# Own transfer for the first scale vector, down weights in two transfers per expert, and activations grouped by half and kind

## What is computed

```python
u = rms_norm(h, norm1_g); proj = u @ w_in                 # w_in: 1024 x 4608
y_conv = conformer_conv(proj[..., :1024], ...)
y_attn = moba_attention(q, k, v, q_norm_g, k_norm_g) @ w_attn_out
g = sigmoid(proj[..., c4:] + b_gates)
h = h + (g[..., :D] * y_conv + g[..., D:] * y_attn) @ w_out
u2 = rms_norm(h, norm2_g); top_v, top_i = top_k(u2 @ w_router + b_router, 4)
# for each expert e and the tokens routed to it:
    t = u2[tok] @ w_ug[e] + b_ug[e]                       # 1024 -> 2048
    a = minimum(t[:, :1024], 7); lin = clip(t[:, 1024:], -7, 7)
    act = a * sigmoid(1.702 * a) * (lin + 1)
    h[tok] += gate * (act @ w_down[e] + b_down[e])        # 1024 -> 1024
```

## Time and profile before

| | us |
|---|---|
| median of three runs | 1130.43 |
| lowest and highest | 1129.95, 1130.46 |
| the profiled execution's own time | 1127.98 |
| its span | 1126.2 |
| PE busy | 967.3 |
| DVE busy | 393.8 |
| ACT busy | 309.8 |

### The profile page before, as it was taken

How to read it: one execution, slowest core, us unless ns; L and a number is a source line. 1 busy time by engine, 2 the same in 40 slices (tenths; PEclk the granted TensorE clock), 3 DMA queues, 4 the chain that set the end, 5 groups by cost and what they waited for, 6 DMA issues and landing times.

```text
span 1126.2 us, 19760 instructions
## 1 busy us (share of the span) xinstructions
PE 967.3 (86%) x7261; PEld 445.8 (40%) x7262; DVE 393.8 (35%) x1014; ACT 309.8 (28%) x534; POOL 5.3 (0%) x27
## 2 busy tenths in 40 slices
PE   6999899998666769899996799998996976998667
PEld 5998689632211213233331233332332321332112
DVE  4699966432111112223232133322322321232111
ACT  4565573222111111212221122221221211222111
POOL 1000000000000000000000000000000000000000
PEclk8999999999888898999998899998999998999887
DMA  7473259999999999999999999999999999999996
GB/s 270 169 290 122 103 182 402 387 414 425 425 427 426 427 428 426 427 425 426 427 427 425 428 425 426 425 428 425 426 425 427 427 426 427 426 427 429 425 427 250
DMA packets 50918, 432.97 MB, mean 384 GB/s; under 512 B 4845, under 2 KB 5265, under 8 KB 18128
## 3 DMA queue, kind: packets, MB, share of 16 engines
q1 hardware_dynamic: 50424, 432.50, 92.3%
q10 hardware_dynamic: 472, 0.16, 0.1%
HBM read 431.59 MB, written 1.05 MB: 384 GB/s over the span
## 4 chain that ended last, share of the span: by engine, by line
PE 48%; DMA 24%; SPq 20%; DVE 4%; issue 2%; ACT 1%; DVEq 0%; ACTq 0%
PE bank L1312 16%; SPq L404 12%; DMA up_odd<-in_w_up_gate 10%; DMA up_even<-in_w_up_gate 10%; PE bank L1043 9%; PE bank L1346 8%; SPq L410 6%; PE bank L1234 5%; DMA down_even<-in_w_down 3%; PE bank L1303 3%; PE bank L1281 2%; DVE up_odd L723 2%; PE bank L1073 1%; PE bank L1332 1%; DVE w_lo L698 1%
## 5 line engine op out<-in xcount | busy, mean ns | idle before, releaser
L1312 PE MATMUL bank<-up_even,reg_r 128*32 128x512 f32 x1472 | 189.9, 661 | 68.2 <-DMA up_even<-in_w_up_gate 68.2
L1312 PE MATMUL bank<-up_odd,reg_r 128*32 128x512 f32 x1408 | 179.4, 654 | 66.1 <-DMA up_odd<-in_w_up_gate 66.1
L998 DVE TENSOR_TENSOR ys<-reg_m,ys 64x512 fp32r<-64x512 f32 x90 | 61.7, 685 | 236.6 <-ACT ys L650 236.0
L1312 PEld LDWEIGHTS bank<-up_even,reg_r 128*32 128x32 f32 x1472 | 47.0, 115 | 203.6 <-DMA up_even<-in_w_up_gate 103.9
L1312 PEld LDWEIGHTS bank<-up_odd,reg_r 128*32 128x32 f32 x1408 | 44.9, 115 | 194.0 <-DMA up_odd<-in_w_up_gate 99.1
L638 ACT ACTIVATE reg_m<-reg_m 128x256 f32<-128x256 f32 x45 | 18.9, 420 | 370.4 <-DVE reg_m L979 370.4
L1234 PE MATMUL bank<-reg_h,reg_r 128*32 128x256 f32 x736 | 93.2, 636 | 0.7 <-DVE reg_r L869 0.7
L979 DVE TENSOR_SCALAR reg_m<-bank 128x256 f32<-128x256 f32 x45 | 19.1, 425 | 211.7 <-PE bank L1312 211.7
L646 ACT ACTIVATE reg_m<-bank,gslot 128x512 f32<-128x512 f32 x45 | 30.9, 688 | 195.5 <-PE bank L1346 195.5
L1346 PE MATMUL bank<-down_even,reg_r 128*32 128x512 f32 x736 | 84.4, 596 | 0.4
L1346 PE MATMUL bank<-down_odd,reg_r 128*32 128x512 f32 x704 | 80.7, 596 | 0.5 <-DMA down_odd<-in_w_down 0.5
(11 more groups left out here) (252 smaller groups left out, 1188.1 us busy)
## 6 DMA issues: line engine op xcount, KB each, us to landing
up_even<-in_w_up_gate SPq DMA_DIRECT2D x64, 2048.0 KB, 35.8
up_odd<-in_w_up_gate SPq DMA_DIRECT2D x64, 2048.0 KB, 38.5
down_even<-in_w_down SPq DMA_DIRECT2D x64, 1024.0 KB, 36.5
down_odd<-in_w_down SPq DMA_DIRECT2D x64, 1024.0 KB, 36.5
down_even<-in_w_in SPq DMA_DIRECT2D x6, 2048.0 KB, 8.4
down_odd<-in_w_in SPq DMA_DIRECT2D x2, 2048.0 KB, 8.7
down_odd<-in_w_in SPq DMA_DIRECT2D x4, 512.0 KB, 8.5
down_odd<-in_w_attn_out SPq DMA_DIRECT2D x1, 2048.0 KB, 8.0
```

The source lines that it names most:

```text
L998: ins = nc.vector.tensor_tensor(ys[64:P, half, :], YR[r, :], ys[0:64, half, :].bitcast(F32), ALU.subtract)
L1312: ins = mm(UP[q * SLOTS:(q + 1) * SLOTS, :], XT[:, k % 2, k // 2 * SLOTS:(k // 2 + 1) * SLOTS], up_columns(a, k, q), start=False, stop=(k ...
```

## The change

It has five parts.

1. norm1_g goes straight into a tile of its own, g1c, 8 values per partition, by the first transfer of ACT's queue, with its own semaphore. The tile par keeps the other eight transfers; four of them are issued behind the pieces of group 0, and PE's transposes and DVE's copies of them move behind group 0's first half.
2. Feature 8p + k lies at partition p, position k: w_in is loaded so (eight neighbouring rows per partition), and x is transposed with a stride of 8.
3. Only the first 256 columns of group 0 stay plain fp32. The other 256 are split into high and low parts and use the three products.
4. Four neighbouring rows of the down weights lie on one partition. In the loop they come as two transfers of 2 MB, 16 KB per partition; for the first two experts still as four of 1 MB.
5. In UP, partitions 0 to 63 hold the first 1024 columns (two groups of 512) and partitions 64 to 127 the linear half. The elementwise steps run over 64 partitions by 512, the sigmoid's result goes to UP in PSUM, and PE transposes four blocks of which half the columns are used.

The diff, without unchanged lines and without the renumbered columns of par:

```diff
@@ -50,6 +50,8 @@
+DOWNS = 2
+DOWNK = KD // DOWNS
@@ -147,9 +149,10 @@
-        ACT_A, ACT_B, ACT_C = [REG_M[:, 256 * i:256 * i + 256] for i in range(3)]
+        ACT_AC = REG_M[:, 0:512]
+        ACT_A, ACT_C = ACT_AC[0:64, :], ACT_AC[64:P, :]
-        actT = REG_R[:, 896:1152].rearrange("p (j s) -> p j s", j=2)
+        actT = REG_R[:, 896:1152].rearrange("p (r s) -> p r s", r=4)
@@ -203,17 +207,18 @@
...
+        ACT_B = UP[0:64, :]
         def up_columns(a, k, q):
-            return up[a][:, k, :].rearrange("p (g f) -> p g f", g=2)[:, :, 256 * q:256 * q + 256]
+            return up[a][:, k, 512 * q:512 * q + 512]
@@ -265,7 +270,7 @@
-        win = w_in.rearrange("(k p) n -> p k n", p=P)
+        win = w_in.rearrange("(p k) n -> p k n", k=KD)
@@ -330,18 +335,12 @@
-            sp.dma_start(dwr, conv_dw).then_inc(par_in, 16)
-            sp.dma_start(rows[8:24, :], b_gates.rearrange("(r c) -> r c", c=P)).then_inc(par_in, 16)
-            for r, src in ((36, q_norm_g), (37, k_norm_g)):
-                sp.dma_start(rows[r:r + 1, :].rearrange("r (h d) -> r h d", h=2),
-                             src.rearrange("(r h d) -> r h d", r=1, h=1).to_broadcast([1, 2, HD])).then_inc(par_in, 16)
-            def down_part(a, c):
-                return (DOWN_EVEN, DOWN_ODD)[a][:, 2 * D * c:2 * D * c + 2 * D]
+            def down_part(a, c, n):
+                return (DOWN_EVEN, DOWN_ODD)[a][:, n * c:n * c + n]
@@ -349,8 +348,9 @@
             def load_down(a, c, e):
-                sp.dma_start(down_part(a, c), w_down[e, 2 * c * P:(2 * c + 2) * P, :].rearrange("(p r) n -> p (r n)", r=2)
-                             ).then_inc(down_in[a][c], 16)
+                h, r = c // 2, c % 2 * 2 * D
+                sp.dma_start(down_part(a, c, 2 * D), w_down[e, DOWNK * h * P:DOWNK * (h + 1) * P, :].rearrange("(p r) n -> p (r n)", r=DOWNK)[:, r:r + 2 * D]
+                             ).then_inc(down_in[a][h], 16)
@@ -358,13 +358,17 @@
+                    sp.dma_start(dwr, conv_dw).then_inc(par_in, 16)
+                    sp.dma_start(rows[0:16, :], b_gates.rearrange("(r c) -> r c", c=P)).then_inc(par_in, 16)
+                    for r, src in ((28, q_norm_g), (29, k_norm_g)):
+                        sp.dma_start(rows[r:r + 1, :].rearrange("r (h d) -> r h d", h=2),
+                                     src.rearrange("(r h d) -> r h d", r=1, h=1).to_broadcast([1, 2, HD])).then_inc(par_in, 16)
                     for q in range(4):
-                        sp.dma_start(bup[q * E:(q + 1) * E, :].rearrange("e (g f) -> e g f", g=2),
-                                     b_up_gate.rearrange("e (g h f) -> e g h f", g=2, h=4)[:, :, q, :]).then_inc(bup_in, 16)
+                        sp.dma_start(bup[q * E:(q + 1) * E, :], b_up_gate[:, 512 * q:512 * q + 512]).then_inc(bup_in, 16)
@@ -405,9 +409,9 @@
             def fetch_down(a, e, items):
-                for c in range(4):
+                for c in range(DOWNS):
-                    sp.dma_start(down_part(a, c), w_down[bass.ds(e, 1), 2 * c * P:(2 * c + 2) * P, :].rearrange("e (p r) n -> p (e r n)", r=2)
+                    sp.dma_start(down_part(a, c, DOWNK * D), w_down[bass.ds(e, 1), DOWNK * c * P:DOWNK * (c + 1) * P, :].rearrange("e (p r) n -> p (e r n)", r=DOWNK)
@@ -476,7 +480,8 @@
-            for r, src, n in ((0, norm1_g, 8), (24, conv_dw_b, 4), (28, conv_ln_g, 4), (32, conv_ln_b, 4)):
+            act.dma_start(g1c[:], norm1_g.rearrange("(p k) -> p k", k=KD)).then_inc(g1_in, 16)
+            for r, src, n in ((16, conv_dw_b, 4), (20, conv_ln_g, 4), (24, conv_ln_b, 4)):
@@ -495,9 +500,14 @@
             def weights_high(i, b):
-                arrived(act, i)
+                if i == 0:
+                    for c in range(4):
+                        act.wait_ge(g0_in[c], 16)
+                else:
+                    arrived(act, i)
+            weights_high(0, 1)
@@ -638,10 +648,10 @@
-                nc.scalar.activation(actT, ACT_T[:, 0:2 * P].rearrange("p (j s) -> p j s", j=2),
+                nc.scalar.activation(actT, ACT_T[:].rearrange("p (r s) -> p r s", r=4)[:, :, 0:2 * SLOTS],
-                act.wait_ge(down_done[3], n + 1)
+                act.wait_ge(down_done[DOWNS - 1], n + 1)
@@ -671,13 +681,9 @@
-            dve.wait_ge(par_full, 1)
-            nc.vector.tensor_copy(par[:], PAR_BANK[:, 0:38]).then_inc(par_ready, 1)
-            nc.vector.tensor_copy(dwT[:], PAR_BANK[:, 64:64 + KC * TAPS].rearrange("p (c w) -> p c w", c=KC)).then_inc(par_ready, 1)
-            dve.wait_ge(par_ready, 2)
+            dve.wait_ge(g1_in, 16)
@@ -694,13 +700,19 @@
-                dve.wait_ge(w_hi_ready, 2 * (i - 1) + b + 1)
+                dve.wait_ge(w_hi_ready, 2 * i + b)
-            for i in (1, 2):
-                for b in range(2):
-                    weights_low(i, b)
+            weights_low(0, 1)
+            for b in range(2):
+                weights_low(1, b)
+            dve.wait_ge(par_full, 1)
+            nc.vector.tensor_copy(par[:], PAR_BANK[:, 0:30]).then_inc(par_ready, 1)
+            nc.vector.tensor_copy(dwT[:], PAR_BANK[:, 64:64 + KC * TAPS].rearrange("p (c w) -> p c w", c=KC)).then_inc(par_ready, 1)
+            for b in range(2):
+                weights_low(2, b)
+            dve.wait_ge(par_ready, 2)
@@ -976,8 +988,8 @@
-                nc.vector.tensor_scalar(ACT_A, UP[:, 0:256], LIMIT, None, ALU.min).then_inc(clip_ready, 1)
-                nc.vector.tensor_scalar(ACT_C, UP[:, 256:512], LIMIT, -LIMIT, ALU.min, ALU.max).then_inc(lin_ready, 1)
+                nc.vector.tensor_scalar(ACT_A, UP[0:64, :], LIMIT, None, ALU.min).then_inc(clip_ready, 1)
+                nc.vector.tensor_scalar(ACT_C, UP[64:P, :], LIMIT, -LIMIT, ALU.min, ALU.max).then_inc(lin_ready, 1)
@@ -1022,14 +1034,9 @@
-                        ins = nc.tensor.transpose(bank[(U_XT + b) % 4][:, c:c + P], hx[:, m, k * P:(k + 1) * P], ident[:])
+                        ins = nc.tensor.transpose(bank[(U_XT + b) % 4][:, c:c + P], features(m)[:, k, :], ident[:])
-            pe.wait_ge(par_in, 16 * 9)
-            nc.tensor.transpose(PAR_BANK[:, 0:38], rows, ident[0:38, 0:38])
-            for c in range(KC):
-                ins = nc.tensor.transpose(PAR_BANK[:, 64 + c * TAPS:64 + (c + 1) * TAPS], dwr[:, c * P:(c + 1) * P], ident[0:TAPS, 0:TAPS])
-            ins.then_inc(par_full, 1)
@@ -1061,19 +1068,22 @@
-            for b in range(2):
-                u = U_G + b
-                claim(u)
-                for c in range(2):
-                    ch = 2 * b + c
-                    for k in range(KD):
-                        if ch == 0 and k % 2 == 0:
-                            freed(pe, U_XT + k // 2)
-                            pe.wait_ge(g0_in[k // 2], 16)
-                        ins = mm(bank[u % 4][:, c * T:(c + 1) * T], stream[0][1][:, k, ch * P:(ch + 1) * P], uT[:, k, :],
-                                 start=(k == 0), stop=(k == KD - 1))
-                ins.then_inc(bank_full[u % 4], 1)
+            claim(U_G)
+            for c in range(2):
+                for k in range(KD):
+                    if c == 0 and k % 2 == 0:
+                        freed(pe, U_XT + k // 2)
+                        pe.wait_ge(g0_in[k // 2], 16)
+                    ins = mm(bank[U_G % 4][:, c * T:(c + 1) * T], stream[0][1][:, k, c * P:(c + 1) * P], uT[:, k, :],
+                             start=(k == 0), stop=(k == KD - 1))
+            ins.then_inc(bank_full[U_G % 4], 1)
+            pe.wait_ge(par_in, 16 * 8)
+            nc.tensor.transpose(PAR_BANK[:, 0:30], rows, ident[0:30, 0:30])
+            for c in range(KC):
+                ins = nc.tensor.transpose(PAR_BANK[:, 64 + c * TAPS:64 + (c + 1) * TAPS], dwr[:, c * P:(c + 1) * P], ident[0:TAPS, 0:TAPS])
+            ins.then_inc(par_full, 1)
+            channel_group_bank(0, 1)
@@ -1328,8 +1338,8 @@
-                for j in range(2):
-                    ins = nc.tensor.transpose(ACT_T[:, j * P:(j + 1) * P], ACT_A.rearrange("p (f j) -> p j f", j=2)[:, j, :], ident[:])
+                for r in range(4):
+                    ins = nc.tensor.transpose(ACT_T[:, r * P:(r + 1) * P], ACT_AC.rearrange("p (f r) -> p r f", r=4)[:, r, :], ident[:])
@@ -1338,13 +1348,14 @@
-                for c in range(4):
-                    pe.wait_ge(down_in[a][c], 16 * pair + 16)
-                    for j in range(2):
+                for c in range(DOWNS):
+                    pe.wait_ge(down_in[a][c], 16 * pair + 32)
+                    for r in range(DOWNK):
                         for half in range(2):
-                            row = (2 * half + j) * SLOTS
-                            ins = mm(YB[row:row + SLOTS, :], actT[:, j, c * SLOTS:(c + 1) * SLOTS],
-                                     down[a][:, 2 * c + j, half * 512:(half + 1) * 512], start=(c == 0), stop=(c == 3), skip_group_check=True)
+                            row = (2 * half + r % 2) * SLOTS
```

(3 more changed lines are left out.)

19 lines of the change are left out of this document (10 added, 9 removed).

## The result

The changed kernel takes 1118.89 us, the median of four runs (1118.4 to 1119.93), against 1130.19 for the kernel before, four runs beside it (1129.8 to 1130.46): ratio 0.9908, 95% interval 0.9889 to 0.9927, so 8.3 to 12.5 us less. The forecast was 1121.7 with a range from 1118.8 to 1127.0; the time lies inside it, 0.1 us from its lower edge. The profiled execution took 1118.4, span 1116.7, which is 9.6 us under the profiled execution before (1127.98), where the sum said 8.7. A later comparison with more runs gave less: 1119.72 (six runs, 1116.93 to 1123.11) against 1127.53 (eleven runs, 1125.71 to 1133.89), ratio 0.9919 [0.9891, 0.9947]. The ratios rest on all the executions and need not be the quotients of the medians: here the medians differ by 7.8 us, the ratio says 9.1 (6.0 to 12.3).

What follows compares the result with a forecast made beforehand. It took a front bound by the chain of engines, then some 900 us bound by expert-weight delivery. Terms -4.8 - 4.2 + 0.3 = -8.7 gave 1119.3 profiled, 1121.7 against the median of 1130.43; range 1118.8 to 1127.0.

Steps and rivals of the forecast that it cites:

- the sum: Whole kernel: -4.8 for the front, -4.2 for the weight stream, +0.3 for the last tile, together -8.7 us.
- The opening: Front of the kernel: group 1 starts at 25.0 instead of 29.8 us, gaining 4.8 us, bounds 2.7 to 5.2.
- The rival that w_in's new order makes it land later: Front: w_in's new row order lands later; with the low-clock case 2.1 to 2.5 us lost, 1124, together 13%.
- The clock question: Group 0's plain half: if PE's clock stays low until 18.0 us, the front gains 2.7 us, not 4.8.
- the removed wait: Opening: PE no longer waits for the last parameter vector; scale copy at about 8.7 us, 4.15 us earlier.
- the half in three products: Second half of group 0: 48 fp32r matmuls take 5.8 us in place of 7.0.
- The stream: Down weights in the expert loop: 16 KB runs save 0.13 to 0.15 us per expert, 30 experts, 4.2 us.
- The upper bound of 6.3: Down weights: 126 MB at 419 against 428 GB/s from the DMA windows, 300 less 294 us.
- The estimate of 1.7 us: Down weights: about 3 overhead cycles per packet, 3 in 256 beats against 3 in 512, 0.6% of down time.
- The tile: Expert loop: DVE chain 1.04 us longer but covered; four transposes add 0.2 to 0.34 us per tile, hidden by the queue.
- Near 724: End of the multi-tile experts' run: 4.1 us of queued work, 1.7 remaining after the change, so nothing is lost.
- The end: Last tile: the added transposes stand open once, costing 0.3 us.

Runs made afterwards that it cites:

- wait_par: Changed kernel with parameter transfers, transposes and copies ahead of group 0 again, norm1_g keeping its own transfer; 1121.26 us, ratio 0.9945 to the kernel before.
- after_again: The changed kernel run once more without edit beside the kernel before; 1119.72 us, ratio 0.9919.
- runs8: Changed kernel with its 2 MB down transfers cut into two of 1 MB with 8 KB runs; 1123.16 us, ratio 0.9954 to the kernel before.
- big8: Kernel before plus parts 1 to 3, down weights in two 2 MB transfers per expert with 8 KB runs; 1124.51 us, ratio 0.9972.
- tile_1: Changed kernel with one unused 512-column fp32 multiply more per tile, 0.86 us; 1123.22 us, ratio 0.9958 to the kernel before.
- front_only: Kernel before plus parts 1 to 3 alone, down rows and column groups as before; 1122.65 us, ratio 0.9959.
- up2: Changed kernel with the loop's up weights in two 4 MB transfers of 32 KB runs, not four of 2 MB; 1120.09 us, ratio 0.9934 to the kernel before.
- g0_plain: Changed kernel with part 3 undone, all of group 0 as plain fp32 multiplies; 1119.85 us, ratio 0.9931 to the kernel before.

## Why the prediction was right

**The opening** went as worked out. Scale copy 8.92 (said 8.7), u_lo done at 17.06 (16.7), w_lo at 19.26 (19.1), second half of group 0 from 19.36 to 25.1 (19.2 to 25.0), group 1 at 25.0 (25.0). Two readings in it were too short and did no harm. PE's first multiply came 0.75 later than said (10.36, not 9.6): it follows the start of the scalings by 0.98, as it did before (13.31 to 14.29 in the earlier trace rows), and 0.45 had been allowed; the 1.44 us of waiting for w_lo took this up. And 0.8 was put for two matmuls whose row says 1.22; the copy came only 0.2 late, as they could start at 7.75. The last piece of group 0 landed at 12.27 (13.1 said). In four of the ten traces PE waited 0.4 to 1.2 us for such a piece, always ahead of the wait for w_lo, so it stayed hidden. The rival that w_in's new order makes it land later falls: group 1 landed at 20.82 where it had 20.70 before, and in eight of the ten traces at 20.9 or earlier.

The clock question came out on the good side by luck: the prediction put all 16 multiplies at the upper pace, though before the first 3.7 us had the lower, and gave no reason for it. The 16 multiplies took 7.14 (as t = 0.44 said) or ran at that pace with a wait in between in nine of the ten traces, and 9.97 in wait_par. Of the prices of the parts, that of the removed wait is read from the traces, 2.5 to 3.9 us at the first up multiply; that of the half in three products is not told apart from nothing. And the 4.8 is rather low than high: nine of the ten traces reach the first up multiply 4.4 us or more earlier than the kernel before, and after_again 4.0; the median of the ten is 5.4.

**What was not foreseen** is 0.5 us at the end of the routing: the lead was still 4.8 us at 213 and 5.3 at the first up multiply. Before, PE's granted clock was 0.66 from 215 to 220; after, it was 1.00 in that stretch. Nothing of the change acts there, and other traces scatter by more.

**The stream**: 4.2 said, 4.65 measured in landings (30 x 0.155), and confirmed by runs8 and big8 as a price of the run. The term was undersized by a tenth since PE's starts gave 9.93 and 9.80 and the landings give 9.94 and 9.79. The upper bound of 6.3 from the windows' 419 and 428 GB/s was not reached; a window of 8 us counts packets by their starts and is a rougher measure than the landings. The estimate of 1.7 us that the prediction worked out from the Trainium skill (DMA: Bandwidth & Descriptors, section Why small descriptors are slow) is too small here by more than half; the traces have 10 to 12.5 ns per run.

**The tile**: four transposes take 0.25 us more (1101.29 to 1101.88, 0.59 against 0.34 in the earlier trace rows), between the 0.2 and 0.34 said, and the longer chain on DVE stayed covered: in the tile at 626 us the last product ended at 629.1, PE's gather at 629.9. Tiles now follow at 15.85 us, 15.60 before. Near 724 2.7 us of work were left, 1.7 said. The error was to the safe side, in part because the tiles grew by 0.25 and not by 0.34. That it did not matter is luck in part as well: the margin rests on PE's clock behind the last landing, which in tile_1 took 2.0 us of such a margin by itself.

**The end**: +0.3 said, +0.49 in the trace. The transposes are 0.25 of it. The rest is PE's pace in the last up piece: it took 3.55 us in the changed kernel (above), 3.23 before, and 1.92 in front_only, whose end is 1.1 us shorter than the changed kernel's. The lines of the kernel before and of front_only:

```profile
1104.15 3.23 PE L1312 MATMUL bank<-up_odd,reg_r 128*32 128x512 f32 x16 [1.94 <-DMA up_odd<-in_w_up_gate]
```

```profile
1098.72 1.92 PE L1318 MATMUL bank<-up_odd,reg_r 128*32 128x512 f32 x16 [1.50 <-DMA up_odd<-in_w_up_gate]
```

**The sum** was 8.7 and the profiles gave 9.6. Terms by measurement: opening 4.8 and 0.5 of scatter, stream 4.65, end -0.5, 9.5 in all. So the mechanism is right term by term, and no step failed. The time itself is a weaker witness. The medians gave 11.3 in one comparison and 7.8 in the other, on either side of the forecast 8.7, and 0.1 us faster the changed kernel would have left the range: that it lies inside is partly luck.

## What to carry to other kernels

Where a stream of weights sets the time, look at the length of the contiguous run on each partition before the number of transfers: 8 to 16 KB gave 1.5% of the down time, 16 to 32 KB another 0.8% of the up time, and halving the transfers alone gave nothing. Large pieces are safer in the middle: with all of them large the gain in pace was lost again (up2), since the queue ran dry once and 32 multiplies instead of 16 stood behind the last up landing, at a granted clock of 0.59. And before adding to a loop that the stream hides, count the work left in the queue at its worst place, and leave room for PE's clock; here 0.86 us more per tile cost about 4 us, not 39.

Where single executions scatter by some us, compare landings and stretches over all the traces at hand: the 4.65 us of the stream stand clear in nine traces, where the times of two kernels could hardly tell them apart.

## What the runs showed of the hardware

- Transfers to 64 partitions, 1 MB in 16 KB runs, brought the queue to 277 GB/s, with 16 KB packets of 901 ns in the mean against 615; two halves took 9.6 us where a full 2 MB takes 4.9, and the kernel 1689 us instead of 1119. The cause stays open.
- PE multiplies of the opening ran at two paces, 6 and 11 records per 2 us, in traces whose granted clock is 1.00 in both stretches (g0_plain: 10 to 16 us and 18 to 26 us; wait_par likewise), while before the slow stretch had 0.50. So the granted clock on record does not tell this pace in every trace.
- The landing of one 2 MB group, issued at the same moment behind the same bytes, was 20.82 in one execution of the same kernel and 22.16 in another, and with PE's clock behind it that was 2.8 us at the first tap (45 us) and 1.3 at the first up multiply.
- Behind a wait of 1.61 us for a landing PE did 16 multiplies in 1.92 us at a granted clock of 1.00 (changed kernel, 624 us), and behind one of 1.85 us at the same place in 3.64 us at 0.50 (tile_1), where the clock stayed low for 6 us.
